# First norm of a two-layer diffusion transformer: shift columns out of the tile path, biases made in the sixth product, three scales on VectorE

## The reference, cut to what matters

```python
def rmsnorm(x, g):
    xf = x.astype(jnp.float32)
    y = xf * lax.rsqrt(jnp.mean(xf * xf, -1, keepdims=True) + NORM_EPS)
    return (y * g.astype(jnp.float32)).astype(x.dtype)

def modulate(h, g, shift, scale):
    return rmsnorm(h, g) * (1 + scale) + shift

def adaln_terms(s, w, b):
    return jnp.split(jax.nn.silu(s) @ w + b, N_MOD, -1)

def swiglu(x, w_up, w_down):
    gate, up = jnp.split(x @ w_up, 2, -1)
    return (jax.nn.silu(gate) * up) @ w_down
...
        ml = adaln_terms(c[:, None, :], ada_w[i], ada_b[i])
        mc = adaln_terms(c_ctx, ada_w[i], ada_b[i])
        h = h + 0.5 * ml[2] * swiglu(modulate(h, norm_g[i, 0], ml[0], ml[1]), ffn_w_up[i, 0], ffn_w_down[i, 0])
```

## Time and profile before

| | us |
|---|---|
| median of 3 runs | 3075.9 |
| the profiled execution, its span | 3074.0 |
| PE busy | 2973.5 |
| DVE busy | 1600.5 |
| ACT busy | 983.4 |
| POOL busy | 996.1 |

### The profile page before, as it was taken

One profiled execution on the slowest core, in us unless ns is written; L12 is line 12 of the kernel. 1 busy time (PEld: TensorE's weight loads), 2 busy tenths in 40 slices (PEclk: granted clock), 3 DMA queues, 4 the chain that ended last, 5 costly groups with the idle time before them and its releaser, 6 DMA issues.

```text
span 3074.0 us, 45849 instructions
## 1 busy us (share of the span) xinstructions
PE 2973.5 (97%) x19023; PEld 2784.3 (91%) x19023; DVE 1600.5 (52%) x2437; ACT 983.4 (32%) x1700; POOL 996.1 (32%) x516
## 2 busy tenths in 40 slices
PE   6999999999999988999999999999999999999998
PEld 6999999999888876899999999999999877798997
DVE  6556666884646665576667783212123358431223
ACT  4211212343454456321121233212123247532222
POOL 5333333333332202233333332222222222344442
PEclk8999999999999999999999999999999999999999
DMA  4434444223320022234334331211211210132221
GB/s 190 141 114 135 122 141 138 89 85 120 115 68 15 8 87 77 89 112 149 126 130 142 121 117 64 69 56 63 68 61 50 81 42 2 63 101 92 90 96 70
DMA packets 126236, 284.25 MB, mean 92 GB/s; under 512 B 40222, under 2 KB 57550, under 8 KB 126030
## 3 DMA queue, kind: packets, MB, share of 16 engines
q1 hardware_dynamic: 123150, 274.86, 27.4%
q10 hardware_dynamic: 2880, 6.47, 0.5%
HBM read 269.68 MB, written 15.10 MB: 93 GB/s over the span
## 4 chain that ended last, share of the span: by engine, by line
PE 89%; DVE 5%; ACT 4%; issue 2%; POOL 0%; DMA 0%; ACTq 0%; SPq 0%; DVEq 0%; POOLq 0%
PE psum L1788 78%; PE psum L1962 2%; PE psum L2062 2%; PE psum L2050 1%; DVE o_acc L1618 1%; PE psum L2043 1%; PE psum L1947 1%; ACT prob_o L1269 1%; PE psum L2003 1%; DVE prob_o L1719 1%; PE psum L1982 1%; PE psum L1969 1%; PE psum L1992 0%; DVE probT_o L1731 0%; ACT cacc L1122 0%
## 5 line engine op out<-in xcount | busy, mean ns | idle before, releaser
L893 POOL TENSOR_TENSOR wl<-raw,wh 128x1024 fp32r<-128x1024 f32 (+1 forms) x329 | 838.2, 2548 | 1643.8 <-ACT wh L998 1642.6
L1788 PE MATMUL psum<-uh,wh 128*128 128x256 f32 (+5 forms) x2704 | 660.0, 325 | 24.7 <-DVE ul L1336 17.7
L1788 PE MATMUL psum<-ul,wh 128*128 128x256 f32 (+5 forms) x2704 | 658.6, 325 | 0.0
L1788 PE MATMUL psum<-uh,wl 128*128 128x256 f32 (+5 forms) x2704 | 658.5, 325 | 0.0
L1788 PE MATMUL psum<-ah,wh 128*128 128x386 f32 (+4 forms) x2192 | 596.4, 344 | 5.6 <-POOL wl L893 4.4
L1788 PE MATMUL psum<-ah,wl 128*128 128x386 f32 (+4 forms) x2192 | 591.3, 342 | 0.0
L1788 PE MATMUL psum<-al,wh 128*128 128x386 f32 (+4 forms) x2192 | 589.0, 341 | 0.0
L1788 PEld LDWEIGHTS psum<-uh,wh 128*128 128x128 f32 (+1 forms) x2704 | 450.7, 189 | 48.5 <-issue 21.5
L1540 DVE SCALAR_TENSOR_TENSOR ada_product<-ada_w,cb 128x1024 f32<-128x1024 f32 x256 | 478.1, 1868 | 5.1
L1788 PEld LDWEIGHTS psum<-uh,wl 128*128 128x128 f32 (+1 forms) x2704 | 450.6, 189 | 19.7
L1788 PEld LDWEIGHTS psum<-ul,wh 128*128 128x128 f32 (+1 forms) x2704 | 450.0, 189 | 19.8
(11 more groups left out here) (248 smaller groups left out, 2433.9 us busy)
## 6 DMA issues: line engine op xcount, KB each, us to landing
raw<-in_w SPq DMA_DIRECT2D x264, 512.0 KB, 3.6
ada_w<-in_ada_w SPq DMA_DIRECT2D x128, 512.0 KB, 3.6
raw<-in_w SPq DMA_DIRECT2D x64, 448.0 KB, 3.4
spill<-cacc ACTq DMA_DIRECT2D x16, 384.0 KB, 2.6
scale_w<-in_scale_w SPq DMA_DIRECT2D x8, 512.0 KB, 13.6
ada_start<-in_ada_w SPq DMA_DIRECT2D x8, 512.0 KB, 14.4
ada_w<-bias_final SPq DMA_DIRECT2D x16, 256.0 KB, 3.0
h<-in_xT SPq DMA_DIRECT2D x8, 384.0 KB, 13.8
```

Source lines behind the costliest of these rows:

```text
L893: nc.gpsimd.tensor_tensor(wl[n % SPLIT_SLOTS][:, 0:k * w], raw[n % RAW_SLOTS][:, 0:k * w], wh[n % SPLIT_SLOTS][:, 0:k * w].bitcast(f32), A ...
L1788: ins = nc.tensor.matmul(pair[0:w, lo:hi], wt[n % SPLIT_SLOTS][:, k * w:(k + 1) * w], xt[:, k, cols], start=first, stop=last)
```

## The change

The shift columns leave the tile path. The first six products (`early`: gate 0, up 0, gate 1, up 1, gate 2, up 2) are made over 768 columns, without the two shift columns. A new item "bias" before up 2 stands for their biases: in the middle of up 2, ahead of its tile 4 (`BIAS_AT`), PE multiplies the weights of all six with a small tile shift_x [128, 8, 4] that holds the high and low parts of the two shifts, 96 matmuls with 4 or 2 columns moving, into bank 7. DVE copies them into the two end columns of each product's tile (`copy_bias`), and only then do ACT and DVE finish gates and ups. The weights of the first three products have buffers of their own (start_wh, start_wl) until then, so that those of six products are there at once; ah lies over them later.

The eight shift chunks are now all on DVE, for both c: two before the norm's reciprocal, three after the first three products are scaled, three after up 1 is scaled. POOL's and ACT's part (`context_shift`, L1175) and POOL's sum of squares are gone; DVE adds the squares. The first three low splits go from POOL to DVE (`low_split`). c over all partitions now comes by a broadcast transfer and a Silu on ACT, not from PE. Of the eight scales PE makes those of tiles 0, 1, 2, 4, 6; those of 3, 5, 7 are summed on DVE (`start_scale`, twice 1024 elements each). The shift columns of the other norms are written with two instructions instead of sixteen.

```diff
+EARLY = 6
+PE_SCALES = (0, 1, 2, 4, 6)
+CHUNKS_BEFORE_NORM, CHUNKS_BEFORE_FOURTH = 2, 5
+BIAS_AT = 4
...
+    s = insert_before([("start",)] + late(0, ffn_products(0, 0), FUSED), ffn_products(0, 0)[EARLY - 1], [("bias",)])
...
         scale_w = [tb(f"scale_w{i}", [P, D]) for i in range(KD)]
-        ada_start = [tb(f"ada_start{i}", [P, D]) for i in range(ADA_FIRST)]
+        ada_start = [tb(f"ada_start{i}", [P, D]) for i in range(2)] + ada_w[0:2] + scale_w[0:4]
...
             load_start(0)
+            load_raw(0)
+            load_start(1)
             load_raw(FUSED - 1)
-            for k in range(KD):
-                if k:
-                    load_start(k)
-                sp.dma_start(ada_start[k][:, :], a["ada_w"][ada_order[k]]).then_inc(start_loaded[k], 16)
+            load_start(2)
+            sp.dma_start(cb[:, :, :].rearrange("p v d -> p (v d)"), a["c_rows"].to_broadcast([P, 2 * D])).then_inc(c_rows_loaded, 16)
+            for k in range(3, KD):
+                load_start(k)
+            for k in range(2):
+                load_ada_start(k)
+            load_raw(FUSED)
...
+            sp.wait_ge(start_gain, 4)
+            for k in range(4, KD):
+                load_ada_start(k)
...
-                    if n >= SPLIT_SLOTS:
-
-                        act.wait_ge(product_done, number[slots[n - SPLIT_SLOTS][0]] + 1)
-                    nc.scalar.activation(wh[n % SPLIT_SLOTS][:, 0:k * w], raw[n % RAW_SLOTS][:, 0:k * w],
+                    if n >= FUSED + SPLIT_SLOTS:
+                        y = slots[n - SPLIT_SLOTS][0]
+                        act.wait_ge(product_done, number[("bias",) if y in early[FUSED:-1] else y] + 1)
+                    nc.scalar.activation(high_weight(n)[:, 0:k * w], raw[n % RAW_SLOTS][:, 0:k * w],
                                          ACT.Copy).then_inc(hi_split, 1)
...
+                elif x[0] == "bias":
+                    act.wait_ge(start_shift, 1)
+                    for v in range(2):
+                        nc.scalar.activation(shift_x[:, :, 1 - v], mod[:, 0, 0, :, v], ACT.Copy)
+                    shift_high(0, uh)
+                    split_up_to(EARLY + 1)
+                    for y in early[:-1]:
+                        finish_product(y)
...
+            def copy_bias(x):
+
+                dve.wait_ge(product_done, number[("bias",)] + 1)
+                dve.wait_ge(scaled, scaled_no[x] + 1)
+                ends, columns, n = out_tile(x)[:, 0:TU:TU - 1], bias_columns(x), 2 * early.index(x)
+                nc.vector.tensor_copy(ends, columns[:, 0:2]).then_inc(bias_copied, 1)
+                dve.wait_ge(bias_copied, n + 1)
+                nc.vector.tensor_tensor(ends, columns[:, 2:4], ends, ALU.add).then_inc(bias_copied, 1)
...
+            def start_scale(k):
+
+                n = 2 * (k - sum(q < k for q in PE_SCALES))
+                dve.wait_ge(tile_loaded[k], 32)
+                dve.wait_ge(c_rows_ready, 1)
+                for v in range(2):
+                    if n + v:
+                        dve.wait_ge(gain_summed, n + v)
+                    nc.vector.scalar_tensor_tensor(out=start_product[:, :], in0=scale_w[k][:, :], scalar=1.0, in1=cb[:, v, :],
+                                                   op0=ALU.mult, op1=ALU.mult,
+                                                   accum_out=mod[:, 0, 1, k, v:v + 1]).then_inc(gain_summed, 1)
...
             for k in range(KD):
                 start_gains(k)
-                if k == 0:
-                    dve.wait_ge(c_rows_made, 1)
-                    nc.vector.tensor_copy(cb[:, 0, :], c_rows(0)).then_inc(c_rows_copied[0], 1)
-                    dve.wait_ge(c_rows_copied[0], 1)
-                ada_chunk(ada_order[k])
+                for n in ((0,), (1, 2))[k] if k < 2 else ():
+                    low_split(n)
                 late_low(norm_items[0], k)
-                start_shifts(k)
-                dve.wait_ge(shift_hi, k + 1)
-                shift_low(0, k).then_inc(shift_lo, 1)
-            dve.wait_ge(c_rows_copied[1], 1)
+                if k:
+                    add_square(0, k - 1)
+                if k + 1 < KD and k + 1 not in PE_SCALES:
+                    start_scale(k + 1)
+            add_square(0, KD - 1)
+            for c in ada_order[:CHUNKS_BEFORE_NORM]:
+                ada_chunk(c)
...
+                            if m:
+                                finish_product(y)
+                            else:
+                                scale_product(y)
+                    if m == 0:
+                        for c in ada_order[CHUNKS_BEFORE_NORM:CHUNKS_BEFORE_FOURTH]:
+                            ada_chunk(c)
+                elif x[0] == "bias":
+                    shift_low(0)
+                    for y in early[:FUSED + 1]:
+                        copy_bias(y)
+                    for y in early[1:-1]:
+                        finish_product(y)
+                elif x == early[FUSED]:
+                    scale_product(x)
+                    for c in ada_order[CHUNKS_BEFORE_FOURTH:ADA_FIRST]:
+                        ada_chunk(c)
+                    start_shifts()
...
+            def early_biases():
+
+                pe.wait_ge(scaled, scaled_no[early[FUSED]] + 1)
+                pe.wait_ge(shift_lo, 1)
+                for y in early:
+                    n, bank = slot_of[y], bias_columns(y)
+                    for k in range(KD):
+                        nc.tensor.matmul(bank, high_weight(n)[:, P * k:P * k + P], shift_x[:, k, :], start=k == 0, stop=False)
+                        ins = nc.tensor.matmul(bank[:, 0:2], low_weight(n)[:, P * k:P * k + P], shift_x[:, k, 0:2],
+                                               start=False, stop=k == KD - 1)
+                ins.then_inc(product_done, 1)
```

More of the change, by code:

```diff
@@ L72, in over @@
             plan.setdefault(chosen[len(chosen) * c // len(chunks)], []).append(chunk)
[L74 removed]
+    at = [i for i, x in enumerate(items) if x[0] in ("gate", "up", "down") and x[1:3] == (0, 0)][EARLY - 1:]
     n = next(k for k, i in enumerate(at) if items[i][0] == "down")
@@ L235, in build @@
     late_proj = {l: [x for x in late_items if x[0] == "proj" and x[1] == l] for l in range(DEPTH)}
-    fused = ahead[0]
+    fused, early = ahead[0], [x for x in late_items if norm_of(x) == 0][:EARLY]
     with ExitStack() as ctx:
@@ L429, in released @@
                 return [(start_gain, KD)]
+            if kind == "bias":
+                return [(bias_copied, 2 * EARLY)]
             if kind in RESIDUAL:
@@ L475, in build @@
                 place[x] = (4, 1)
+            elif kind == "bias":
+                place[x] = (7, 1)
             elif kind in ("vt", "start"):
@@ L498, in start_bank, with bias_columns, high_weight, low_weight @@
         def start_bank(k):
-            return banks_of(("start",))[:, 512 * (k % 2):512 * (k % 2) + 2]
-        def c_rows(v):
-            return psum[:, D * v:D * v + D]
+            b = PE_SCALES.index(k) % 2
+            return banks_of(("start",))[:, 512 * b:512 * b + 2]
+        def bias_columns(x):
+            return banks_of(("bias",))[:, 4 * early.index(x):4 * early.index(x) + 4]
+        def high_weight(n):
+            return start_wh[n] if n < FUSED else wh[n % SPLIT_SLOTS]
+        def low_weight(n):
+            return start_wl[n] if n < FUSED else wl[n % SPLIT_SLOTS]
         def segs_of(x):
@@ L736, in _ @@
             sp.dma_start(conv_w[:, :, :], a["conv_w"]).then_inc(const_loaded, 16)
+            for k in range(2, 4):
+                load_ada_start(k)
+            sp.wait_ge(start_gain, 4)
+            for k in range(4, KD):
+                load_ada_start(k)
             sp.dma_start(rpb_s[0:120, :], a["rpb"]).then_inc(rpb_loaded, 16)
@@ L882, in _ @@
             nc.gpsimd.memset(rstd[:, TU - 1:TU], 1.0).then_inc(ones_set, 1)
-            done = [0]
+            done = [FUSED]
             def split_up_to(n_slots):
@@ L1059, in late_high @@
                     act.wait_ge(mod_ready, mod_terms(x, 0, 1))
-                    for k in range(KD):
-                        ins = shift_high(m, k, high)
-                    ins.then_inc(shift_hi, 1)
+                    shift_high(m, high)
                 for v, (lo, hi) in enumerate((LAT, CTX)):
@@ L1343, in late_low @@
                 if m and q == 0:
-                    dve.wait_ge(shift_hi, KD + late_no[m])
-                    for k in range(KD):
-                        ins = shift_low(m, k)
-                    ins.then_inc(shift_lo, 1)
+                    shift_low(m)
                 dve.wait_ge(late_hi, KD * late_no[m] + q + 1)
@@ L1536, in ada_chunk @@
                     w, product = ada_w[n % ADA_BUFS], ada_product
-                for v in range(2 if n >= ADA_FIRST else 1):
+                if n == 0:
+                    dve.wait_ge(gain_summed, 2 * (KD - len(PE_SCALES)))
+                for v in range(2):
                     if on_dve(n) + v:
@@ L1785, in dense_step @@
                 K, w = slots[n][1:]
```

(10 more changed lines are left out.)

167 lines of the change are left out of this document (82 added, 85 removed).

## The result

| | before | after |
|---|---|---|
| median, us | 3075.8 (3070.9 to 3077.0) | 3089.6 (3086.6 to 3091.1) |
| ratio, 95% interval | | 1.0048 (1.0035 to 1.0061) |
| profiled span, us | 3074.0 | 3085.7 |
| up 1 (u1) begins, us | 77.27 | 56.12 |
| up 3 (u3) begins, us | 111.1 | 123.28 |

The changed kernel is slower by 13.8 us. The forecast was +2.6, in a range from 3068 to 3088; the measured time lies 1.6 us above the range.

What follows compares the result with a forecast made beforehand. PE, 97% busy, was taken as the bound, losing time only in the start. Up 3's start moving from 111.1 to 113.0 us (+1.9) plus 0.7 for slow clock gave 3075.9 + 2.6 = 3078.5 us, range 3068 to 3088.

Steps and rivals of the forecast that it cites:

- The start, up to u1: Tile steps before up 1: DVE and the round trip through ACT set the rhythm; up 1 near 52.5, 24.8 us won.
- the gain of tile 2: Anchor of the tile steps in the start: it was to fall near 18.0 us, with DVE through at 48.8.
- DVE's list: DVE's work behind the last tile, from 48.8 us: sums, reciprocal, copies, waits; 36.4 us, shifts ready at 85.2.
- The exclusion: DVE's shift sums beside POOL's weight splits: two-input DVE products and POOL block each other, 6.2 us.
- The waits of PE: PE idle before gate 2 (3 us), before up 2 (3), inside up 2 (5) and before up 3 (3.2).
- The bias block: 96 narrow matmuls in the middle of up 2: 0.106 each, 10.2 us, plus 1.7 for the clock, ending at 97.1.
- Rival B: In the bias matmuls: the narrow matmul is dear, 0.176 each, block 20.4 us, whole kernel 3087; chance 0.17.
- Its signs: Marks of the dear narrow matmul in the bias block: from 0.14 us each, a block over 13.5 us.
- The rest costs nothing: Other norms, term sums and narrower tiles: covered by matmuls or in DVE's free time; narrower tiles 0.1 us.
- The sum: Up 3 starting at 113.0 instead of 111.1, +1.9, and 0.7 for a partly slow up 3: +2.6 us.
- the clock term: Half speed after PE's 5 us wait for the shifts, added to the bias block: 1.7 us, between 0 and 3.5.
- the split of waits into those under 2 us: PE's clock: full speed kept through waits under 2 us, about half granted after waits of 9.6 and some 4 us.

Runs made afterwards that it cites:

- e6: Changed kernel with the low splits of weight slots 3 and 4 on VectorE instead of GpSimd; ratio 1.0038 to the kernel before.
- e3: Changed kernel with 27 dense matmuls, results unused, put before PE's wait for the shifts; ratio 1.0021 to the kernel before.
- e2: Changed kernel with 6 bias matmuls instead of 96, the rest of these biases left out; 3068.0 us, ratio 0.9979 to the kernel before.
- e5: Kernel before with lone blocks of 48, 96 and 24 narrow matmuls ahead of three gates of the first feed-forward layer; ratio 1.0096 to the kernel before.
- e1: Changed kernel with 64 and 32 columns moving in the bias matmuls instead of 4 and 2; ratio 1.0040 to the kernel before.
- e12: Changed kernel with two low splits on VectorE, all scales on TensorE, 27 filler matmuls, buffers freed early and 48 bias matmuls; ratio 0.9987 to the kernel before.
- e9: Changed kernel with 48 bias matmuls instead of 96, those with the low parts of the weights left out; ratio 1.0007 to the kernel before.

## Why the prediction was wrong

- **The start, up to u1: right in mechanism, 3.6 us too early.** Steps were 3.46 and 6.0 us (3.56 and 6.08 taken), POOL was empty until 51.27. What was off is the anchor: the gain of tile 2 came at 20.8, not 18.0, since the second scale took 3.57 us like the first, and the step behind it, ahead of scale 2, ran at half pace up to 17.8. DVE was through at 51.1 instead of 48.8. PE was granted 0.52 from 31.4 to 34.7 and 0.50 from 49.2 to 51.9, so the norm matmuls began only at 53.7. u1 began at 56.1, above the 51 to 54 I had named. (The forecast's own terms, 48.8 + 1.3 + 0.9, give 51.0; the 1.5 us up to its 52.5 stand in no term.)
- **DVE's list: right.** 36.4 us were taken, 86.2 - 51.1 = 35.1 measured. The exclusion in it was 2.06 + 1.98 + 1.06 = 5.1 us (rows 52.35, 55.74 and one at 67.73 of 2.28) where 6.2 was taken, and e6 shows it by taking the splits away. The trace agrees there with the rule that the prediction names from the Trainium skill, "SBUF — State Buffer", section "Who interferes with whom". The shifts were ready at 86.2, forecast 85.2.
- **The waits of PE: right.** 1.3, 2.5, 4.4 and 2.1 us, where 3, 3, 5 and 3.2 stood. Together 10.3 instead of 14.2. The three ahead of the block are 2.8 us shorter, which makes up for most of the late u1: the block's start hangs on DVE's list, not on PE.
- **The bias block: the step that failed.** I took 0.106 for each, and 1.7 us (0 to 3.5) for the clock. The first is nearly confirmed: 0.109 in e3. The second was mis-sized: the term was 10.3 us in the block (20.5 - 10.2), and 1.6 behind it. The reasoning was at fault, not only the number: I took the clock's loss as something that a wait leaves behind and that passes once PE is busy again, as in the earlier trace rows. In e2 it passes so. In the block it doesn't: the clock stays down as long as these matmuls last, and it falls in them without any wait (e3, e5).
- **Rival B: near by luck.** It had a block of 20.4 us and gave 3087. That the block's length is nearly the measured one is luck: the rival had 0.176 each and a few us of half clock, that is a dear matmul, and e3 shows the matmul to be cheap at full clock. Its signs (from 0.14 each, a block over 13.5 us) were met with 0.213 and 20.5.
- **"The rest costs nothing": holds.** Behind u3, PE's waits for POOL from 140 us on are 8.4 us in 6 times in the changed kernel and 8.6 in 6 in the one before. From u3's start to the end the changed kernel takes 0.5 us less.
- **The sum.** u3 came 10.3 us after its forecast: the block began 1.1 us late, was 8.6 us longer than the 11.9 taken, and u3 began 16.5 us after its end instead of 15.9. Behind u3 the clock cost 1.0 us more than taken and 2.2 came back: 9.1 in the span. The other 2.0 are no step of the forecast: the median lies 3.9 us above the profiled span, where 1.9 was taken.
- **The range** was short because a bound of the clock term (3.5 us) was taken from how long the clock stayed low behind past waits. Its bound should have been the whole block at the other level. With 10.3 instead of 1.7 the forecast would have been 3087.1. The clock's 1.6 us behind the block would add nothing in that sum, since there u3 hangs on its split, 15.9 us after the biases, and not on PE.

What had stood in view before: the kernel before has narrow matmuls at half pace. Its first scale takes twice as long as the one in the earlier trace rows (1.84), 16 in 9.47 - 6.06 = 3.4 us, 0.213 each:

```profile
6.06 3.54 PE L1810 MATMUL psum<-c_cols,scale_w 128*128 128x2 f32 x16 [6.06 <-DMA h<-in_xT]
```

The table of stages says 1.00 in those first microseconds, in both kernels, though the first dense matmuls of the changed one go at half pace too; there only the pace tells. And the split of waits into those under 2 us, behind which PE keeps its clock, and longer ones doesn't hold in the changed kernel. Its clock fell behind the wait of 1.34 us in the row below (0.52 from 31.4 to 34.7), and stayed at 1.00 behind the 2.53 us before u2; behind 2.65 us at the same place in e2 it fell to 0.50.

```profile
30.25 0.62 PE L1862 MATMUL psum<-uh,start_wh 128*128 128x384 f32 x2 [1.34 <-DVE ul L1366]
```

What stays open: which property of a bias matmul it is that the clock answers to, and what decides behind which wait it falls. e1 shows that a 64-column operand doesn't bring the clock back, but I didn't try whether such a block would lower it from full. Nor did I try one narrow to one dense in this kernel itself; there the buffers of slots 6 and 7 must be free before so many dense matmuls have run.

## What to carry to other kernels

A block of matmuls with a full weight load and few columns is to be priced at both levels of the clock, and what stands behind it too: here 96 of them cost 20.5 us and not 10.2 behind a wait, and 16.5 without one. Columns that ride along with a dense matmul are nearly free (in the products from 77.3 to 111 us of the kernel before, those with 384 and those with 386 columns last 0.34 us alike), so taking them out and making them up afterwards was a bad trade here, even though it shortened the start: without most of the block this change is 0.2% faster (e2), with it 0.5% slower. If such matmuls must be, spread them thinly: one to each dense one kept the full clock here, four to one didn't. By an estimate even that wouldn't pay in this kernel: 96 at 0.106 are 10.2 us, more than the 6 to 7 us that the rest of the change gains in e2.

## What the runs showed of the hardware

- The granted clock fell to 0.5 while PE was busy without a gap: in e5 four us into 48 matmuls of 4 columns, in e3 about as far into the block, in e12 2.8 us into it. Even 24 of them (2.6 us) left the dense matmuls behind them at 0.53 for 3.4 us.
- At full clock a weight load with its narrow matmul has a pitch of 0.106 (the fp32 scale in the earlier trace rows; in fp32r the first 16 of e12, 1.70 us) to 0.109 us (e3), at half clock 0.213 (the changed kernel); the loads themselves last 0.19 and 0.33, and overlap. The Trainium skill, "TensorE: Matmul & The Clock Gate", section "Back-to-back issue gap", gives about 81 ns for a load and a matmul of 128 columns. No run here has that form in fp32r; 2 or 4 columns already took more, 106 to 109 ns, so the estimate of 7.8 us that the prediction made from it was too low.
- A moving operand of 64 columns costs no more than one of 4 at half clock (e1: 19.9 us for the block, against 20.5, its first six at full clock).
- Behind such a block, dense matmuls had the full clock back after 3.3 us (the changed kernel), 3.4 (e9) and some 5.6 (e5, the block of 96).
- A VectorE product with two SBUF inputs took 1.22 us alone and 3.2 to 3.3 beside a GpSimd split of 2.4 (e6, and rows 52.35 and 55.74 of the changed kernel).
